# Hybrid decoder step: projections of the scan stage as products of rounded parts, the weights split by transfers

## The chip, the cores and the metric
One core of one Trainium2 chip. The metric is the time of one execution on the device in microseconds (us), lower is better. The engines are called TensorE (PE in the profile, PEld for its weight loads), VectorE (DVE), ScalarE (ACT), GpSimd (POOL) and SyncE (SP). Each works through its own program in order and waits on semaphores.

## The reference
One layer of a hybrid decoder for 512 prompt tokens and 8 x 4 sample tokens, all float32. The input is projected once by `w_in`. Three branches follow (latent attention, a Mamba-2 scan, cross-attention to 256 memory tokens), then a gated merge, and a feed-forward part with 4096 hidden units. The change touches the projections of the scan branch:
```
proj = x @ w_in                     # x: 544 tokens x 1024
z, xbc, dt, ...  = split(proj)      # z: 2048 columns, xbc: 3072
xbc = silu(causal_conv(xbc))        # 4 taps
y, S = ssd(xbc, dt, state)          # chunks of 128 tokens, 4 groups of 8 heads
y = rms_norm_by_group(y * silu(z))
```

## The kernel before, in words
**Layout.** Tokens lie along the free dimension (T = 544, in two halves of HT = 272), features along the 128 partitions. x is `X`, eight chunks of 128 features (KC = 8). The weights come as a stream of 217 blocks of 128 x 1024 (512 KB), in the order in which TensorE uses them (PHASES, line 127; lay_out, line 2441): one for dt, six for the convolution of group 0, then 40 in the stage "ssm" (ten for each of four groups: four of z, six of the next group's xbc, in the last group those of the attention's latents), then mem_k, the heads and so on. SP loads them into `ring`, four slots (load, line 574); a slot is reloaded when TensorE has begun the block after the one in it (`blocks_begun`).

**Two ways of a projection.** `project` (line 1825) multiplies one block with X in float32: 8 chunks x 2 halves, 16 matmuls. `three_products` (line 1840) works with a high part of weights and x, rounded to fp32r, and a low part, the rest: high x high, high x low, low x high, 48 matmuls of a shorter kind. The heads' stage and the merge and feed-forward stages already work by parts: ScalarE rounds a block (round_head_block, line 743), VectorE or GpSimd subtract it from the whole (rest_of_head_block, line 1545; split_block, line 540). The 40 blocks of the scan stage don't.

**The order in the scan stage** is written out by hand on each engine, one loop over the groups each. TensorE (line 2012) has the ten projections in turns with the group's other matmuls: transposes, B by C, states, the read-outs of four pairs of heads (`read_out`), the samples, the state sums (`state_adds`). Blocks are numbered 0 to 9 in a group in what follows: the read-outs stand ahead of blocks 4, 5, 7 and 8. ScalarE (line 829) evacuates z (`z_read`), makes the decays of heads 0 to 7 (`decays`), evacuates the next group's projections (`ahead`), applies tanh (`ahead_silu`) and squares. VectorE (line 1347) convolves, weights the decays (`weigh`), reads the scan's results and adds the sample states (`add_state`). GpSimd (line 478) scales C by the decays (`scale_c`), multiplies eight sample states and sums squares. The rows of cumulated dt come by SP.
```
                for h in range(4):
                    scale_c(h)
                pool.wait_ge(sem["s_off_ready"], t.next("s_off_ready"))
                for b in range(DEC_BATCH):
                    pool.tensor_tensor(by_head(st_s[:, b, :]), by_head(st_s[:, b, :]), heads(dec_s, b, g, P),
                            MUL).then_inc(sem["st_dec_ready"], 1)
                    if b == 3:
                        scale_c(4), scale_c(5)
```

## Time and profile before
| | us |
|---|---|
| median of three timed runs (lowest to highest) | 1672.19 (1671.03 to 1673.26) |
| the profiled execution | 1671.78 |
| its span, first to last instruction | 1669.7 |
| TensorE busy | 1623.7 (97%) |
| VectorE busy | 781.7 (47%) |
| ScalarE busy | 453.3 (27%) |
| GpSimd busy | 407.7 (24%) |

The times come from the whole execution; a profile's rows are of one execution. Busy time of TensorE overlaps from matmul to matmul, so the distance between starts tells more than the mean of one. A row of the timeline merges neighbouring instructions of one line, and its bracket tells how long the engine stood idle before it and what released it. "issue" is time in which it waited for nothing that the profile shows. A float32 matmul leaves two records.

### The profile page before, as it was taken

To read this page: it belongs to the slowest core of one execution; us is meant where nothing else is said; L and a number is where in the kernel's file an instruction comes from. 1 tells how busy PE (TensorE), PEld (TensorE's weight loads), DVE (VectorE), ACT (ScalarE), POOL (GpSimd) and SP (SyncE) were. 2 spreads that over 40 slices of the span, in tenths; PEclk is the share of its full clock that TensorE was granted. 3 is DMA by queue.
4 is the path that set the end of the run, shared out by engine and by line. 5 is a ranking of instruction groups with operands and counts; after the bars stand their busy time and mean duration, and the time that the engine had idled before them with its cause. 6 is when DMAs were issued, how large, how long until landed. Compare 5 with 4: busy or idle time off the path is not lost.

```text
span 1669.7 us, 27037 instructions
## 1 busy us (share of the span) xinstructions
PE 1623.7 (97%) x10950; PEld 1408.9 (84%) x10950; DVE 781.7 (47%) x1350; ACT 453.3 (27%) x857; POOL 407.7 (24%) x344
## 2 busy tenths in 40 slices
PE   8999999999999999999999999999988999999995
PEld 6878787787878888888888877789988999999995
DVE  5657676765343222223333223253488751077234
ACT  2252433425332222222122111142234111111122
POOL 0041231403120000001244200124444334444432
PEclk9999999999999999999999999999999999999998
DMA  5424234252362222224788766422322323222221
GB/s 182 160 78 165 95 114 140 84 184 82 101 231 64 76 76 76 64 76 149 255 273 272 247 246 246 174 89 89 93 72 64 89 89 88 86 84 86 88 64 54
DMA packets 71853, 210.62 MB, mean 126 GB/s; under 512 B 10321, under 2 KB 26962, under 8 KB 66866
## 3 DMA queue, kind: packets, MB, share of 16 engines
q1 hardware_dynamic: 51824, 155.99, 29.5%
q10 hardware_dynamic: 13762, 31.93, 5.4%
q0 software_dynamic: 6144, 20.98, 3.5%
q8 instruction: 86, 1.41, 0.3%
q14 instruction: 37, 0.30, 0.1%
HBM read 194.01 MB, written 14.86 MB: 125 GB/s over the span
## 4 chain that ended last, share of the span: by engine, by line
PE 84%; DVE 7%; ACTq 3%; ACT 2%; issue 2%; DMA 1%; SPq 0%; POOL 0%; DVEq 0%
PE acc L1902 30%; PE acc L1835 21%; PE acc L1848 9%; PE acc L2208 4%; PE acc L2171 3%; PE acc L2154 2%; ACTq L1014 1%; ACTq L1012 1%; PE bank L2222 1%; PE bank L2241 1%; PE bank L2223 1%; DVE work L1303 1%; PE bank L2294 1%; PE bank L2326 1%; PE bank L2189 1%
## 5 line engine op out<-in xcount | busy, mean ns | idle before, releaser
L1835 PE MATMUL acc<-xt,ring 128*128 128x272 f32 x1504 | 358.9, 395 | 0.0
L1835 PEld LDWEIGHTS acc<-xt,ring 128*128 128x128 f32 x1504 | 282.4, 190 | 67.7 <-issue 12.0
L1902 PE MATMUL acc<-x_parts,f_parts 128*128 128x272 f32 x1408 | 219.6, 291 | 10.7 <-DVE x_parts L1230 6.2
L544 POOL TENSOR_TENSOR f_parts<-ring,f_parts 128x1024 fp32r<-128x1024 f32 x65 | 158.5, 2439 | 247.2 <-ACT f_parts L764 247.0
L1902 PEld LDWEIGHTS acc<-x_parts,f_parts 128*128 128x128 f32 x1408 | 196.0, 191 | 13.4 <-issue 6.0
L1902 PE MATMUL acc<-f_parts 128*128 128x272 f32 x1344 | 172.3, 289 | 0.0
L522 POOL DMA_DIRECT2D work<-in_page_cols x128 | 69.0, 539 | 422.2 <-PE bank L2262 382.0
L1902 PEld LDWEIGHTS acc<-f_parts 128*128 128x128 f32 x1344 | 170.4, 188 | 0.1
L1848 PE MATMUL acc<-work_high,high 128*128 128x272 f32 x464 | 138.4, 298 | 0.0
L764 ACT ACTIVATE f_parts<-ring 128x1024 fp32r<-128x1024 f32 x65 | 68.8, 1059 | 239.2 <-PE acc L1902 204.5
L1848 PE MATMUL acc<-work_high,ring_low 128*128 128x272 f32 x464 | 133.8, 288 | 0.0
L1848 PE MATMUL acc<-x_low,high 128*128 128x272 f32 x384 | 110.7, 288 | 0.0
L1848 PEld LDWEIGHTS acc<-work_high,high 128*128 128x128 f32 x464 | 87.2, 188 | 5.7 <-issue 5.3
L1848 PEld LDWEIGHTS acc<-work_high,ring_low 128*128 128x128 f32 x464 | 87.7, 189 | 0.0
L1549 DVE TENSOR_TENSOR ring_low<-ring,high 128x1024 fp32r<-128x1024 f32 x32 | 39.2, 1224 | 86.7 <-ACT high L749 86.4
L1798 DVE TENSOR_SCALAR f_parts<-attended 128x544 fp32r<-128x544 f32 x32 | 76.5, 2390 | 1.1
L1848 PEld LDWEIGHTS acc<-x_low,high 128*128 128x128 f32 x384 | 73.0, 190 | 0.2 <-issue 0.2
L1303 DVE SCALAR_TENSOR_TENSOR work<-work,vecs 128x600 f32<-128x600 f32 x72 | 68.5, 951 | 2.4
L1902 PE MATMUL acc<-f_parts,mg_parts 128*128 128x272 f32 x528 | 68.8, 289 | 0.0
L544 POOL TENSOR_TENSOR mg_parts<-ring,mg_parts 128x1024 fp32r<-128x1024 f32 x21 | 51.0, 2426 | 70.8 <-ACT mg_parts L764 70.8
L1902 PEld LDWEIGHTS acc<-f_parts,mg_parts 128*128 128x128 f32 x528 | 67.3, 188 | 0.2
L1902 PE MATMUL acc<-x_parts,mg_parts 128*128 128x272 f32 x480 | 62.1, 289 | 0.6 <-DVE attended L1792 0.6
(369 smaller groups left out, 2508.7 us busy)
## 6 DMA issues: line engine op xcount, KB each, us to landing
ring<-in_stream SPq DMA_DIRECT2D x216, 512.0 KB, 3.6
work<-in_page_cols POOLq DMA_DIRECT2D x128, 160.0 KB, 5.1
attended<-in_ssm_state ACTq DMA_DIRECT2D x8, 1024.0 KB, 6.3
work<-cum_rows SPq DMA_DIRECT2D x32, 256.0 KB, 4.5
out_ssm_s<-attended ACTq DMA_DIRECT2D x8, 1024.0 KB, 5.6
work<-in_ckv_rows ACTq DMA_DIRECT2D x64, 128.0 KB, 3.6
work<-in_ckv_rows SPq DMA_DIRECT2D x64, 128.0 KB, 2.6
work<-in_memk_cols SPq DMA_DIRECT2D x8, 1024.0 KB, 7.2
```

The source lines that it names most:

```text
L522: pool.dma_start(keys[kq][:, i * KEYS_W:(i + 1) * KEYS_W], page_cols[ids[kq * 4 + i]]).then_inc(sem[f"keys_in_slot{kq}"], 16)
L544: pool.tensor_tensor(lo, ring[:, s * BLOCK:(s + 1) * BLOCK], hi.bitcast(F), SUB).then_inc(sem["split_ready"], 1)
L764: act.activation(hi, ring[:, s * BLOCK:(s + 1) * BLOCK], ACT.Copy).then_inc(sem["hi_ready"], 1)
L1303: dve.scalar_tensor_tensor(out=c, in0=ext[j][:, i:i + CL], scalar=tap(i), in1=c, op0=MUL, op1=ADD).then_inc(sem[signal], 1)
L1549: dve.tensor_tensor(ring_low[:, of], ring[:, of], W_HIGH[i % 2].bitcast(F), SUB).then_inc(sem["split_ready"], 1)
L1798: dve.tensor_scalar(hi, q, 1.0, None, MUL).then_inc(sem["dve_step"], 1)
L1835: m = pe.matmul(acc[p][:, half, 0:width], w[:, k * P:(k + 1) * P], x(kk)[:, half * width:(half + 1) * width], start=kk == 0, stop=kk == n_ ...
L1848: m = pe.matmul(out[:, half, 0:HT], w[:, k * P:(k + 1) * P], x[k][:, of], start=k == 0 and n == 0, stop=last and k == KC - 1 and n == 2)
L1902: m = pe.matmul(acc_half, w[:, k * P:(k + 1) * P], x[:, kk, of], start=kk == 0 and n == 0, stop=kk == last and n == 2)
L2154: m = pe.matmul(acc[p][:, 0, 0:N_MEM], w[:, k * P:(k + 1) * P], mem[:, k, :], start=k == 0, stop=k == KC - 1)
L2171: m = pe.matmul(acc[p][:, half, 0:HT], w[:, c * 256 + off:c * 256 + off + P], cq[:, c, half * HT:(half + 1) * HT], start=c == 0, stop=c == 2)
L2208: m = pe.matmul(acc[1][:, half, 0:HT], w[:, k * P:(k + 1) * P], BR[:, KC + k, half * HT:(half + 1) * HT], start=False, stop=k == KC - 1)
```

## The change
The 40 blocks of the scan stage are multiplied by parts (`project_parts_of_x`). Their weights are split by transfers, which GpSimd issues. Of block i the stream is moved once into a slot of `ring_parts` (fp32r, at the place of `ring`) by a transfer that rounds; ScalarE writes the negative of the rounded block to one of three buffers W_LOW; a second transfer adds the stream to it, which leaves the low part. The adding transfer of block i+2 is issued ahead of the rounding one of block i+3, at ten places in GpSimd's program, and the negations stand at ten places in ScalarE's. x is rounded and its rest subtracted in place at the start of the stage and no more at its end. SP loads nothing into the ring in the stage, and loads mem behind it. Semaphores are merged.
```diff
+            def round_weights(i):
+                at = SSM_AT + i
+                s = at % RING
+                if i < SSM_SPLIT:
+                    pool.wait_ge(sem["blocks_begun"], CREDIT["blocks_begun"] + at - RING + 2)
+                    pool.dma_start(ring_parts[:, s * BLOCK:(s + 1) * BLOCK], stream[at]).then_inc(sem[f"w_rounded{i % 2}"], 16)
+
+            def rest_of_weights(i):
+                if i < SSM_SPLIT:
+                    if i:
+                        pool.wait_ge(sem["w_rest"], 16 * i)
+                    pool.wait_ge(sem["negated"], i + 1)
+                    pool.dma_start(W_LOW[i % 3], stream[SSM_AT + i], accum_op=ADD).then_inc(sem["w_rest"], 16)
+
+            def weights_ahead(g, q):
+                i = g * (GC + QC) + q
+                rest_of_weights(i + 2)
+                round_weights(i + 3)
+
+            round_weights(0)
+            rest_of_weights(0)
+            round_weights(1)
+            rest_of_weights(1)
+            round_weights(2)
             for g in range(GROUPS):
...
                 pool.wait_ge(sem["const_loaded"], 2 * 16)
+                weights_ahead(g, 0)
                 pool.wait_ge(sem["conv_ready"], t.next("conv_ready", QC))
...
+                weights_ahead(g, 1)
+                weights_ahead(g, 2)
                 pool.wait_ge(sem["cb_read"], t.next("cb_read"))
...
+                weights_ahead(g, 3)
                 for h in range(4):
                     scale_c(h)
+                weights_ahead(g, 4)
                 pool.wait_ge(sem["s_off_ready"], t.next("s_off_ready"))
...
                     if b == 3:
                         scale_c(4), scale_c(5)
+                weights_ahead(g, 5)
                 scale_c(6), scale_c(7)
+                weights_ahead(g, 6)
                 pool.wait_ge(sem["sq_ready"], t.next("sq_ready", 2))
                 pool.tensor_tensor(zc[0], zc[0], zc[1], ADD).then_inc(sem["pool_step"], 1)
+                weights_ahead(g, 7)
+                weights_ahead(g, 8)
...
                 pool.tensor_tensor(sq_sum, zc[0], zc[2], ADD).then_inc(sem["sq_added"], 1)
+                weights_ahead(g, 9)
...
+            block_at.next(SSM_SPLIT)
+            load(3)
+            begun_behind(SSM_AT + SSM_SPLIT - 2)
+            sp.dma_start(mem, mem_t).then_inc(sem["mem_loaded"], 16)
...
+            def negate(i):
+                s = (SSM_AT + i) % RING
+                if i < SSM_SPLIT:
+                    act.wait_ge(sem[f"w_rounded{i % 2}"], 16 * (i // 2 + 1))
+                    if i >= 3:
+                        act.wait_ge(sem["blocks_begun"], CREDIT["blocks_begun"] + SSM_AT + i - 3 + 2)
+                    act.activation(W_LOW[i % 3], ring_parts[:, s * BLOCK:(s + 1) * BLOCK].bitcast(F), ACT.Copy,
+                            scale=-1.0).then_inc(sem["negated"], 1)
...
+                negate(first + 2)
                 z_read(0)
+                negate(first + 3)
...
                 z_read(1)
+                negate(first + 4)
                 z_read(2)
+                negate(first + 5)
...
                 z_read(3)
+                negate(first + 6)
...
                 ahead(0)
+                negate(first + 7)
                 act.wait_ge(sem["y_ready"], t.next("y_ready"))
                 decays(4)
                 decays(5)
...
                 decays(6)
                 ahead(1)
+                negate(first + 8)
                 decays(7)
...
                 ahead(2)
+                negate(first + 9)
                 ahead_silu(2)
                 ahead(3)
+                negate(first + 10)
                 square(2)
...
                 ahead(4)
+                negate(first + 11)
                 square(3)
...
             conv(0, 4)
             finish(0, 3)
...
+            for c in range(KC):
+                if c < KC - 1:
+                    dve.wait_ge(sem["x_read"], c + 1)
+                else:
+                    dve.wait_ge(sem["acc0_ready"], 1 + QC // 2)
+                rest_of_chunks(XL, X, XH, (c,))
             conv(0, 5)
             finish(0, 4)
...
+            def project_parts_of_x(p, between=None):
+                pe.wait_ge(sem[f"acc{p}_free"], t.next(f"acc{p}_free"))
+                s, i = (used.next() - 1) % RING, split_in_ssm.next() - 1
+                pe.wait_ge(sem["w_rest"], 16 * (i + 1))
+                w_high, w_low = ring_parts[:, s * BLOCK:(s + 1) * BLOCK], W_LOW[i % 3]
+                three_products(acc[p], w_high, w_low, XH, XL, True, 0, None if i else "low_even")
+                if between:
+                    between()
+                m = three_products(acc[p], w_high, w_low, XH, XL, True, 1)
+                m.then_inc(sem[f"acc{p}_ready"], 1)
```

## Rows read from the trace of the kernel before

**Rows 1.** The page: busy us, share of the span and instructions of each engine.
```profile
PE 1623.7 (97%) x10950; PEld 1408.9 (84%) x10950; DVE 781.7 (47%) x1350; ACT 453.3 (27%) x857; POOL 407.7 (24%) x344
```

**Rows 2.** Stages, one group: busy us (count) by engine, granted clock, DMA share, GB/s.
```profile
257.50:355.80 98.30, 97.56 (x554) 76.73 (x553) 70.20 (x119) 38.42 (x86) 25.23 (x21) 1.00 0.36 122
```

**Rows 3.** Waits in that group: engine, line, releaser, us in total, times, longest.
```profile
POOL work L508 <- ACT work L902: 21.0, 1, 21.0
ACT work L838 <- PE acc L1835: 19.1, 4, 7.3
```

**Rows 4.** Timeline of TensorE, ahead of the first read-out (start, us, line, shape, [idle before]).
```profile
297.42 0.66 PE L2075 MATMUL bank<-work 128*64 128x128 f32 x8 [0.56 <-DVE work L1401]
```

**Rows 5.** Timeline of TensorE: two and a half float32 projections, and what follows.
```profile
246.50 18.50 PE L1835 MATMUL acc<-xt,ring 128*128 128x272 f32 x80
264.83 1.08 PE L2008 MATMUL bank<-work,cst 128*128 128x272 f32 x4
```

**Rows 6.** Timeline of TensorE in the feed-forward stage: two projections by parts.
```profile
1339.80 12.24 PE L1902 MATMUL acc<-x_parts,f_parts 128*128 128x272 f32 x96
1351.88 6.20 PE L1902 MATMUL acc<-x_parts,mg_parts 128*128 128x272 f32 x48
```

**Rows 7.** Landing: ring loads (512 KB), mem (1024 KB); GpSimd's issues (ns) and landing (160 KB).
```profile
DMA to landing us min/median/max: 3.4/3.6/12.3
...
DMA to landing us min/median/max: 4.9/4.9/4.9
...
L522 POOL DMA_DIRECT2D work<-in_page_cols x128: 536/538/707, 480.2 to 941.5; - x128
...
DMA to landing us min/median/max: 2.7/5.1/8.2
```

**Rows 8.** ScalarE's rounding (ns min/median/max); the group's scalings (busy, mean ns); timeline.
```profile
L749 ACT ACTIVATE high<-ring x32: 1041/1049/1062, 499.9 to 957.6; 128x1024 fp32r<-128x1024 f32 x32
...
L494 POOL TENSOR_TENSOR work<-work 128x384 f32<-128x384 f32 x8 | 8.8, 1102 | 17.7 <-ACT work L858 17.7
...
309.39 1.27 ACT L854 ACTIVATE work<-work 128x128 f32<-128x128 f32 x4
...
313.47 0.51 ACT L858 ACTIVATE work<-work 128x384 f32<-128x384 f32 x1
...
314.06 1.21 POOL L494 TENSOR_TENSOR work<-work 128x384 f32<-128x384 f32 x1 [1.02 <-ACT work L858]
315.23 4.50 POOL L500 TENSOR_TENSOR attended<-attended,work 128x512 f32<-128x512 f32 x4
```

**Rows 9.** Timeline of GpSimd: the sums of squares at a group's end.
```profile
251.70 1.49 POOL L508 TENSOR_TENSOR work<-work 128x544 f32<-128x544 f32 x1 [20.92 <-ACT work L902]
253.27 1.76 POOL L512 TENSOR_TENSOR work<-work 128x544 f32<-128x544 f32 x1
```

**Rows 10.** The DMA view of the same group: all that moved.
```profile
DMA packets 3598, 11.98 MB, mean 122 GB/s; under 512 B 640, under 2 KB 640, under 8 KB 3072
```

**Rows 11.** Timeline of VectorE: last convolution of group 0; four low parts of x.
```profile
60.04 0.18 DVE L1313 SCALAR_TENSOR_TENSOR branch<-work 128x32 f32<-128x32 f32 x1
...
63.20 0.17 DVE L1291 TENSOR_SCALAR work<-work 128x3 f32<-128x3 f32 x1 [2.77 <-ACT work L781]
...
64.12 2.60 DVE L1303 SCALAR_TENSOR_TENSOR work<-work,vecs 128x600 f32<-128x600 f32 x3
...
460.62 2.62 DVE L1543 TENSOR_TENSOR x_low<-xt,work_high 128x544 fp32r<-128x544 f32 x4
```

**Rows 12.** Timeline: two weightings, two state sums; TensorE's block 7 begins.
```profile
326.43 1.29 DVE L1401 TENSOR_TENSOR work<-work 128x512 f32<-128x512 f32 x2
327.64 1.28 DVE L1462 TENSOR_TENSOR attended<-attended,bank 128x512 f32<-128x512 f32 x2
...
330.24 3.83 PE L1835 MATMUL acc<-xt,ring 128*128 128x272 f32 x16
```

**Rows 13.** Timeline of TensorE: what follows the stage's last projection.
```profile
453.28 2.92 PE L1873 MATMUL bank<-work,cst 128*128 128x272 f32 x12
```

More of the change, by code:

```diff
@@ L143 @@
 HEAD_SPLIT = len(SPLIT_AT)
+SSM_AT = blocks_before("ssm")
+SSM_SPLIT = GROUPS * (GC + QC)
 def loaded_before(block, slot):
-    return len(range(slot, block, RING))
+    return sum(not SSM_AT <= at < SSM_AT + SSM_SPLIT for at in range(slot, block, RING))
 CREDIT = {"acc0_free": 1, "acc1_free": 1, "blocks_begun": 8, "keys_used": 4,
@@ L278, in program @@
         ext, cacc, th = ([k(EXT) for _ in range(2)] for _ in range(3))
-        krope, a_rstd = k(T), k(T)
-        late_sq = [k(T) for _ in range(2)]
-        k_rstd = late_sq[0]
+        low_at = k.at
+        krope = work[:, low_at:low_at + T]
+        x_high_at = low_at + BLOCK
+        k.at = low_at + 4 * T
+        assert x_high_at + 2 * T <= k.at
         after_conv = k.at
@@ L289, in program @@
         bc = [k(2 * T).rearrange("p (c t) -> p c t", t=T) for _ in range(2)]
+        cum_at = k.at
         cum_r = [k(SEQ) for _ in range(4)]
+        a_rstd, k_rstd = (work[:, cum_at + i * T:cum_at + (i + 1) * T] for i in range(2))
         b_last = work[2 * NS:NS3, k.at:k.at + P]
@@ L312, in program @@
         xw_full = xdt[NS:2 * NS, NB, :]
-        mem = k(KC * N_MEM).rearrange("p (c m) -> p c m", m=N_MEM)
+        x_high_too_at = k.at
+        k(3 * T)
+        mem = spare[:, 0:KC * N_MEM].rearrange("p (c m) -> p c m", m=N_MEM)
+        mem_again = work[:, xdt_at:xdt_at + KC * N_MEM].rearrange("p (c m) -> p c m", m=N_MEM)
         decay = [xw[:, c, :] for c in range(NB)]
@@ L359, in program @@
         for_heads = k.at
-        a_sq = [bc[0][:, 0, :], bc[0][:, 1, :], late_sq[0], late_sq[1], work[:, b_tm_at:b_tm_at + T]]
+        a_sq = [bc[0][:, 0, :], bc[0][:, 1, :], *(work[:, late_sq_at + i * T:late_sq_at + (i + 1) * T] for i in range(2)),
+                work[:, b_tm_at:b_tm_at + T]]
+        assert late_sq_at + 2 * T <= cum_at - 4 * T
         q_n = k(T)
@@ L794, in latent @@
                 act.activation(a_sq[i], dst, ACT.Square).then_inc(sem["squares_ready"], 1)
+            for c in range(0, KC, 2):
+                act.wait_ge(sem[f"x{c // 2}_loaded"], 32)
             evac(1)
+            round_chunks(XH, X, range(2))
             evac(0)
@@ L805, in _ @@
                               ssm_state[0][:, 4 * i:4 * i + 4, :]).then_inc(sem[f"st{i}_loaded"], 16)
-            act.dma_start(mem, mem_t).then_inc(sem["mem_loaded"], 16)
+            round_chunks(XH, X, range(2, 4))
             evac(0)
             silu(1)
-            act.wait_ge(sem["wb_ready"], t.next("wb_ready"))
+            negate(0)
+            round_chunks(XH, X, range(4, 6))
+            act.wait_ge(sem["cum_ready"], 2)
             act.activation(wb_tm[:, 0:NB, :], wb_tm[:, 0:NB, :], ACT.Exp)
@@ L813, in _ @@
             act.activation(dec_s, bank[0][:, 0:DEC_BATCH * SSM_HEADS].rearrange("p (b h) -> p b h", h=SSM_HEADS),
-                    ACT.Exp).then_inc(sem["dec_ready"], 1)
+                    ACT.Exp).then_inc(sem["exps_ready"], 1)
             evac(1)
+            round_chunks(XH, X, range(6, KC))
+            negate(1)
             silu(0)
@@ L1345, in _, with rest_of_chunks @@
             finish(0, 3)
+            def rest_of_chunks(low, whole, high_parts, cs):
+                for c in cs:
+                    dve.wait_ge(sem["rounded"], t.next("rounded"))
+                    dve.tensor_tensor(low[c], whole[:, c, :], high_parts[c].bitcast(F), SUB).then_inc(sem["low_even"], 1)
+            for c in range(KC):
[4 more added lines that the diff above has]
+                rest_of_chunks(XL, X, XH, (c,))
             conv(0, 5)
@@ L1534, in variance @@
                 m.then_inc(sem[signal], 1)
-            variance(a_rstd, lambda half: bank[half], "cq_summed", Q_LORA, "var_ready")
+            variance(a_rstd, lambda half: bank[half], "latent_summed", Q_LORA, "var_ready")
             group_var()
-            variance(k_rstd, lambda half: acc[0][:, half, :], "ckv_summed", KV_LORA, "var_ready")
-            def rest_of_chunks(low, whole, high_parts, cs):
-                for c in cs:
-                    dve.wait_ge(sem["rounded"], t.next("rounded"))
-                    dve.tensor_tensor(low[c], whole[:, c, :], high_parts[c].bitcast(F), SUB).then_inc(sem["low_even"], 1)
+            variance(k_rstd, lambda half: acc[0][:, half, :], "latent_summed", KV_LORA, "var_ready")
             def rest_of_head_block(i):
@@ L1839, in project @@
                                 m.then_inc(sem["blocks_begun"], 1)
+                            elif half and read and k < KC - 1:
+                                m.then_inc(sem[read], 1)
+                m.then_inc(sem[f"acc{p}_ready"], 1)
[8 more added lines that the diff above has]
+                m = three_products(acc[p], w_high, w_low, XH, XL, True, 1)
                 m.then_inc(sem[f"acc{p}_ready"], 1)
@@ L2061, in _ @@
                 states(0, 1)
-                project(0, of_x, between=lambda: states(2, 3))
+                project_parts_of_x(0, between=lambda: states(2, 3))
                 def read_out(hp):
```

127 lines of the change are left out of this document (60 added, 67 removed).

## The prediction

> **What bounds the kernel now.** I read the page first: TensorE is busy for 97% of the span [rows 1]. Then the stretch of the change, the scan stage (four groups of ten projections), by the view of stages: one group lasts 98.3 us, TensorE is busy for 97.5 of them, VectorE for 70, ScalarE for 38, GpSimd for 25, and the DMA engines for 0.37 [rows 2]. The granted clock is 1.00, the 2.4 GHz level. So here the stage lasts as long as TensorE's work, and every other engine waits: GpSimd up to 21.0 us at a time, ScalarE 19.1 us in a group for z's projections [rows 3]. TensorE itself waits once in a group, 0.56 us, for VectorE's weighting of the decays [rows 4].
>
> **The matrix products.** Two and a half plain projections in a row take from 246.50 to 264.83 [rows 5]: 7.33 us for one of 16 float32 matmuls (each has two records). Two projections as three products of parts, 96 matmuls, take from 1339.80 to 1351.88 [rows 6]: 6.04 us for one. Forty projections so save 40 x 1.29 = 51.6 us of TensorE's time. That is the most the change can bring. What it puts at stake is the supply of the weights, which today is one plain load per block, 3.6 us to landing against a block time of 9.8 [rows 7].
>
> **The new supply, as a chain.** Per block GpSimd issues two software transfers (one rounds 512 KB into ring_parts, one adds the same 512 KB to the negated copy), and ScalarE negates in between. Their order on GpSimd is: wait for `negated(i)`, add(i), round(i+1). ScalarE's negate(i+1) waits for round(i+1). So add(i) cannot start before negate(i), round(i+1) stands behind it on one queue, and negate(i+1) behind that: from one negation to the next it takes L + 1.3 us. L is the time from the issue of the adding transfer to the landing of the rounding one behind it. 1.3 is the negation (ScalarE took 1.05 us to round a block of the same size) and 0.25 for three hand-overs, of about 0.08 each (ScalarE's exponential ends 313.98, GpSimd starts 314.06) [rows 8]. Three buffers allow the chain to run ahead, but never make it quicker than one block in L + 1.3.
>
> **What else stands in that chain.** Both engines work in program order, and the new steps stand between old ones. Per group:
> - between negations 5 and 6: negation 6 waits until block 4 has begun, and block 4 stands behind decays 0 and 1, their scaling and the first read-out: 0.4 + 4.6 + 1.1 + 1.7 = 7.8, which is 1.3 more than L if L is 6.5;
> - between 6 and 7: round(7) stands behind scale_c(3) on GpSimd, that behind decays 2 and 3 on ScalarE, these behind negate(6). A pair of decays takes 4.6 us (309.39 to 313.98), a scaling 1.1 on average [rows 8]: 5.7 us;
> - between 7 and 8: decays 4 and 5 (4.6 us), scale_c(5) 1.2, and then the last four state products, 4.5 us, before weights_ahead(5) issues round(8): 10.3 us [rows 8];
> - between 8 and 9: decay 7 and scale_c(7), 2.3 + 1.2 = 3.5 us;
> - between 11 and 12: square(3) 0.7, the sums 1.5 + 1.7 on GpSimd: 3.9 us [rows 9].
> Together 24.7 us. With ten steps of L + 1.3 a group takes **10 L + 37.7** us, wherever that is above what TensorE needs. What TensorE needs is 98.3 - 12.9 = 85.4, plus 0.7 for the wait on VectorE (its part from the read-outs of states 2 and 3 to the weighted decays is fixed work, so half a projection less of cover makes the 0.56 longer): 86.1.
>
> **Bounds of L.** The trace has no adding and no rounding transfer. Rows near it: 512 KB land in 3.6 us, 1024 KB in 4.9 with nothing beside, so 512 KB more cost 1.3 and the fixed part is 2.3; a 160 KB transfer issued by GpSimd landed at best in 2.7, which is the same 2.3 with its issue [rows 7]. If a transfer that adds moves no more than a plain one, the pair is 1 MB: L = 2.3 + 2.6 = 4.9. If reading the old values counts as much again, the pair is 1.5 MB: 2.3 + 3.9 = 6.2. The stage also moves 11.98 MB in a group, 5.24 of it the loads that the pairs replace [rows 10]; the other 6.7 MB are some 17 us of 98, so the data part grows by about a quarter: 5.5 and 7.2. Nothing excludes that the arithmetic itself is slower than plain copying; by no row can I bound that above, and I let it reach 8. I take 6.6, nearer to the upper case, since `accum_op` has to fetch the old contents and the rounding one shares its queue.
> The Trainium skill, Collectives: The Full Stack, section "The bandwidth ceiling", says that a transfer with a reduction runs at half the rate of a copy, because both sources are read on one ring, and not because the addition costs time. No row here shows it; by it L would be the 7.2 of the paragraph above.
> The Trainium skill, SBUF — State Buffer, warns in its note on "DVE blocks DMA" that GpSimd can't write descriptors while VectorE holds the port pair they share. The issues that the trace shows took 0.54 us at the median and 0.71 at most, so here it would add 0.2 us to an issue, 8 us over 40 blocks at the most, inside the bounds of L.
>
> **The sum.** Start: VectorE makes the low parts of x behind finish(0,3), which ends at 60.2; eight of 0.66 us (2.62 for four) end at 65.5, so the last convolution of the first group starts there instead of at 63.2 and its last tap ends at 69.0; tanh 0.7 and the negation give 71.0 for negate(2) of group 0 [rows 11]. TensorE waits for the same: the low parts cost it some 1 us at its first block, the convolution about as much behind it, both inside the 71.0. Then three groups, 3 x (10 L + 37.7); then from negate(2) to negate(8) of the last, 6 L + 7.8 + 1.3 + 5.7 + 10.3 = 6 L + 25.1 (six steps of L + 1.3, and the first three of the extras); then VectorE: decay 7 to its exponential 1.9, its weighting 0.65, two state sums 1.25, two matmuls 0.6 = 4.4 us to block 7 (VectorE has weigh(7) ahead of add_state(0), for which TensorE waits) [rows 12]; then blocks 7 to 9, 330.24 to 355.80 less 3 x 1.29 = 21.7. The stage's projections end at 36 L + 235.3. They end at 453.28 now [rows 13]. With L = 6.6 that is 472.9: **19.6 us later**. Zero is at L = 6.05.
>
> **Edits at nothing.** The 40 ring loads leave SP's queue; behind them stand the loads of the cumulated rows, which can only come earlier. The load of mem leaves ScalarE's queue for SP's, behind the last block's begin; needed 7 us later, and 1024 KB land in 4.9 [rows 7]; if the queue is full it costs up to 2. The rounding of x at the end (ScalarE 2.9 us, VectorE 3.2) stood beside TensorE's sums behind 453.28 and its mem_k blocks: removed for nothing. The parts of BR move under the same blocks; 8 x 0.66 on VectorE at their end, first needed 20 us later. The second load of mem and shared semaphores change no order that matters. If each of these costs 1 us, that is 3, within the range.
>
> **Base.** The profiled execution ran 1671.8 us with a span of 1669.7; the median of the three timed runs is 1672.2. The forecast is 1671.8 + 19.6 = 1691.4.
>
> **Rivals.**
> 1. The other side: adding costs little more than copying, L of 4.9 to 5.9, and the time is below now. At L = 5.5 the sum gives 1671.8 - 20 = 1652; below 5.4 the chain stops counting in part (from negate(8) the way over block 7, 8, 9, the evacuation and the convolution to negate(12) is 34 us whatever L). One mechanism, one point: L under 6.05. For it: the DMA engines are busy for only 0.37 of the stage now [rows 2]. Against: every old transfer of the stage shares them. 0.25.
> 2. The supply is hidden whole: L under 4.6, or GpSimd and ScalarE run further ahead than I think. Then TensorE's 86.1 per group rules: 51.6 - 4 x 0.7 - 2.5 at the start = 46 us saved, 1626; with some rest 1640. Against: a pair needs 4.9 by the cheapest rows. 0.10.
> 3. The transfers with arithmetic are much slower than plain ones, L of 8 to 10: 1742 to 1814. No row speaks for or against. 0.15.
> 4. L between 6.0 and 6.15: no difference that counts. 0.06.
> 5. That the change doesn't do what it says (the transfer doesn't round, so the parts are no parts) would alter results, not this time: the matmuls and transfers are the same.
>
> **How the numbers follow.** Forecast, L of 6.15 to 7.6 (1675 to 1728): 0.44. A measurement of this kernel tells 0.2%, 3.3 us, from no change. Faster is rivals 1 and 2, 0.35; same 0.06; slower the forecast and rival 3, 0.59. The two signs share the chance, so the range reaches from the middle of the fast cases, 1640, to L of 8, 1743, and leaves out most of rival 2 and the tail of 3. The likeliest case's own range is 1675 to 1728.
>
> **What would show it.** Matmuls of the stage 126 ns apart where they run: 6.04 per block. Right if TensorE's idle time before blocks 4 to 9 is released by DMA or by VectorE's state sums, ScalarE's longest waits are for the rounding transfer ahead of its negations, GpSimd's for the negation, and a group lasts about 104 us. Wrong if groups last 86 to 90 with no idle time on TensorE (L small), if the landing of the adding transfer alone is above 7 us (L large), if the granted clock falls in the gaps (a cost that I have at nothing, as it stays at 1.00 over the present gaps), or if the idle time sits at conv_ready, which would make VectorE the bound.

## The result, and the profile after

The changed kernel took 1728.78 us (median of 4 runs, 1727.48 to 1734.93) against 1672.7 us before on the same chip: a ratio of 1.0344, 95% interval 1.0322 to 1.0366. So 56 us slower, where 19.6 were forecast. Slower was the likeliest sign and the range (1640 to 1743) holds the time, but the forecast's own case (to 1728) ends just under it, and the size is nearly three times what the sum gave.

The profiled execution of the changed kernel took 1734.93 us (span 1732.0); it is 6 us above the other three, which lie within 1.3 us of each other. All that follows is read from it. The page, the same parts as [rows 1], with the chain that ended last:
```profile
PE 1602.9 (93%) x11590; PEld 1436.4 (83%) x11590; DVE 799.3 (46%) x1350; ACT 491.3 (28%) x897; POOL 461.7 (27%) x424
...
PE 66%; DMA 12%; issue 6%; ACT 5%; POOL 5%; DVE 4%; ACTq 3%; POOLq 0%; SPq 0%; DVEq 0%
PE acc L1992 29%; DMA ring_parts<-in_stream 11%; PE acc L1938 9%; PE acc L1912 7%; PE acc L2298 3%; PE acc L2261 3%; POOL work L540 2%; PE acc L2244 2%; ACTq L1089 1%; ACTq L1087 1%; ACT work L923 1%; PE bank L2312 1%; POOL attended L548 1%
```
TensorE's share fell from 97% to 93%, and the landing of the rounding transfer is now 11% of the chain. Where the stage's projections end, TensorE's timeline shows the sum that follows them (L1963 here, 453.28 in [rows 13]):
```profile
515.25 1.09 PE L1963 MATMUL bank<-work,cst 128*128 128x272 f32 x4
```
That is 62.0 us later, and the span grew by 62.3 (1669.7 to 1732.0): the loss lies up to the end of this stage. Behind it the time moved by 0.3 us, so what was costed at nothing there cost next to nothing.

The stages of the same kernel, the stretch that answers to [rows 2] (us, then busy us and count of each engine, granted clock, DMA share, GB/s):
```profile
171.00:278.00 107.00, 82.99 (x644) 74.55 (x643) 67.28 (x105) 45.28 (x92) 36.67 (x39) 0.87 0.53 138
278.00:385.00 107.00, 86.19 (x661) 77.88 (x660) 73.17 (x114) 46.39 (x94) 37.41 (x40) 0.90 0.57 150
```
No engine is full now. TensorE has 21 to 24 us of idle time in 107, and its granted clock, 1.00 before, is 0.87 and 0.90. Who waits for whom, from 60 to 530 us (engine, what waits, releaser, us in total, times, longest):
```profile
ACT high L835 <- DMA ring_parts<-in_stream: 127.5, 22, 9.9
POOL high L509 <- ACT high L835: 118.1, 16, 11.3
...
ACT work_high L835 <- DMA ring_parts<-in_stream: 61.9, 11, 8.8
POOL work_high L509 <- ACT work_high L835: 57.4, 8, 8.9
...
PE bank L2165 <- POOL work L540: 30.9, 4, 8.7
...
PE bank L2206 <- DVE attended L1548: 24.0, 7, 10.4
```
ScalarE's negations (L835) wait for the rounding transfer, GpSimd's adding transfers (L509) for the negation: the chain of the forecast. TensorE hardly ever waits for a weight itself. It waits for the read-out's scaled C (L2165) and for the state sums (L2206), because ScalarE's decays and GpSimd's scalings stand in program order behind the transfers' steps. From negation 2 to 12, to 22 and to 32 the groups last 113.8, 115.8 and 113.6 us, where about 104 were forecast.

Two steps of that chain, from negation 19 to negation 21 of 40. First GpSimd's queue (L509 adding, L502 rounding), then ScalarE's (L835 negation):
```profile
270.82 0.90 POOL L509 DMA_DIRECT2D high<-in_stream  x1 [7.67 <-ACT high L835]
271.42 0.86 POOL L502 DMA_DIRECT2D ring_parts<-in_stream  x1
279.01 0.88 POOL L509 DMA_DIRECT2D high<-in_stream  x1 [6.73 <-ACT high L835]
```
```profile
269.20 1.06 ACT L835 ACTIVATE high<-ring_parts 128x1024 fp32r<-128x1024 f32 x1 [7.71 <-DMA ring_parts<-in_stream]
...
277.41 1.06 ACT L835 ACTIVATE high<-ring_parts 128x1024 fp32r<-128x1024 f32 x1 [2.00 <-DMA ring_parts<-in_stream]
...
279.00 0.35 ACTq L891 DMA_DIRECT2D out_ssm_s<-attended  x1
...
287.76 1.06 ACT L835 ACTIVATE work_high<-ring_parts 128x1024 fp32r<-128x1024 f32 x1 [3.98 <-DMA ring_parts<-in_stream]
```
Negation at 269.20, adding transfer 1.62 later at 270.82, next negation 6.59 after that: a step of 8.21 us with nothing beside it. The next step begins at 277.41; at 279.00 a 1 MB store of the states starts beside it, and the negation comes 8.75 us after the adding transfer. These two are the two kinds of step that the stage has. L, from the adding transfer's start to the landing of the rounding one behind it, read so for the 36 steps from negation 2 to negation 38: 6.56 to 6.81 us in 17 of them (the quiet ones in what follows), 7.07 to 9.53 in the others, **7.49 in the mean**.

### The profile page after: what moved, and what is told of

Its sections match the earlier page's. It is cut to its first block, busy times and chain, and to the rows that moved or that the text cites. A ratio compares the mean times of both kernels' runs of the same rounds, so it can differ in the third digit from the quotient of the medians.

```text
span 1732.0 us, 28478 instructions
## 1 busy us (share of the span) xinstructions
PE 1602.9 (93%) x11590; PEld 1436.4 (83%) x11590; DVE 799.3 (46%) x1350; ACT 491.3 (28%) x897; POOL 461.7 (27%) x424
## 4 chain that ended last, share of the span: by engine, by line
PE 66%; DMA 12%; issue 6%; ACT 5%; POOL 5%; DVE 4%; ACTq 3%; POOLq 0%; SPq 0%; DVEq 0%
PE acc L1992 29%; DMA ring_parts<-in_stream 11%; PE acc L1938 9%; PE acc L1912 7%; PE acc L2298 3%; PE acc L2261 3%; POOL work L540 2%; PE acc L2244 2%; ACTq L1089 1%; ACTq L1087 1%; ACT work L923 1%; PE bank L2312 1%; POOL attended L548 1%; PE bank L2331 1%; PE bank L2313 1%
## 5 line engine op out<-in xcount | busy, mean ns | idle before, releaser
L1938 PE MATMUL acc<-work_high,ring_parts 128*128 128x272 f32 x768 | 225.8, 294 | 0.0
L1938 PE MATMUL acc<-x_low,ring_parts 128*128 128x272 f32 x640 | 191.4, 299 | 0.0
L1938 PE MATMUL acc<-work_high,high 128*128 128x272 f32 x628 | 184.4, 294 | 0.0
L1938 PEld LDWEIGHTS acc<-work_high,ring_parts 128*128 128x128 f32 x768 | 149.4, 194 | 0.6 <-DVE x_low L1425 0.4
L1938 PEld LDWEIGHTS acc<-x_low,ring_parts 128*128 128x128 f32 x640 | 128.4, 201 | 2.3 <-issue 1.2
L1938 PEld LDWEIGHTS acc<-work_high,high 128*128 128x128 f32 x628 | 121.0, 193 | 0.0
L1938 PE MATMUL acc<-high,ring_parts 128*128 128x272 f32 x256 | 82.4, 322 | 4.7 <-DMA high<-in_stream 2.7
L1630 DVE TENSOR_TENSOR ring_parts<-ring,high 128x1024 fp32r<-128x1024 f32 x32 | 39.2, 1224 | 88.5 <-ACT high L800 88.2
L835 ACT ACTIVATE high<-ring_parts 128x1024 fp32r<-128x1024 f32 x26 | 27.6, 1060 | 135.8 <-DMA ring_parts<-in_stream 127.5
```

The lines of the kernel that those rows point to most:

```text
L1630: dve.tensor_tensor(ring_parts[:, of], ring[:, of], W_HIGH[i % 2].bitcast(F), SUB).then_inc(sem["split_ready"], 1)
L1938: m = pe.matmul(out[:, half, 0:HT], w[:, k * P:(k + 1) * P], x[k][:, of], start=k == 0 and n == 0, stop=last and k == KC - 1 and n == 2)
```

## The experiments

"End" is the time at which the stage's projections end in a run's profile (453.28 before, 515.25 changed; elsewhere the first weight load of the same sums, which reads 515.1 in the changed kernel). Mean L and the other terms are over the same 36 steps throughout. A time given as of one run has no interval; the four runs of the changed kernel lie 7 us apart.

**Which price makes L.** Three runs change one size each.

The second transfer doesn't add:
```
-  pool.dma_start(W_LOW[i % 3], stream[SSM_AT + i], accum_op=ADD)
+  pool.dma_start(W_LOW[i % 3], stream[SSM_AT + i])
```


> The changed kernel, with the second transfer of each block writing rounded weights in place of adding to the negated ones (the low parts are then wrong: the addition is left out, all transfers, waits and bytes written stay). Theory A1, the sum of reading and writing back in an adding transfer is a large term of L: L falls from 6.6 (quiet) by 1 to 2 us, the whole by 36 times that: 1655 to 1695 us. Rival A2, an adding transfer costs what a rounding one does: L within 0.3 us of 6.6, 1720 to 1740.

Measured: 1688.52 us (one run), end 470.8. Quiet steps have L = 5.0 to 5.3 (changed kernel: 6.6 to 6.8), the mean is 5.99 in place of 7.49. Theory A1 in its size: adding, in place of writing the rounded weights, costs some 1.6 us of a quiet step. Whether the fetching of the old contents or the arithmetic takes them, the run does not tell. The sum of L fell by 54.0 us and the end by only 44.3, since the waits behind the landings, nearly all for TensorE (a buffer becomes free when a block has begun), grew from 11.7 to 22.9 us in all.

The adding transfer moves half a block:
```
-  pool.dma_start(W_LOW[i % 3], stream[SSM_AT + i], accum_op=ADD)
+  pool.dma_start(W_LOW[i % 3][:, 0:BLOCK // 2], stream[SSM_AT + i][:, 0:BLOCK // 2], accum_op=ADD)
```


> The changed kernel, with the adding transfer moving only the first half of each block's columns (256 KB in place of 512; the other half of the low parts stays the negated rounded weights). If L is bytes through the engines (two transfers of 512 KB in 6.6 us, some 5 us of it bytes), it falls by a quarter of them, 1.2 to 1.7 us a step: 1670 to 1690 us. If L is the fixed latency of the rounding transfer behind, and the adding one runs beside it, it stays within 0.4 us: 1715 to 1735.

Measured: 1698.39 us (one run), end 483.1; quiet L about 6.1, mean 6.67. Neither case: half of the adding bytes gives 0.5 us of a quiet step, 0.8 of the mean. The two transfers overlap in part, and the one that L ends with is the rounding one.

The transfers by themselves, behind the last work of the kernel before (`one` issues a transfer, `landed` waits for it):
```
+  for _ in range(3):
+      one(parts[0]), landed()
+  for _ in range(3):
+      one(parts[0], accum_op=ADD), landed()
+  ...
+  for _ in range(3):
+      one(parts[0], accum_op=ADD), one(parts[1]), landed()
```


> The kernel before, with transfers alone behind its last store, when every engine is idle (the outputs are the kernel's own): from GpSimd's queue one block each, waited for: three rounding, three adding, one of each of 256 KB; three pairs adding + rounding issued together, three pairs rounding + rounding; then all but the halves again while SyncE's queue loads blocks of 512 KB one after the other into other memory; at the end two plain ones. If the changed kernel's quiet landings (5.4 adding, 6.1 rounding behind it, 6.6 for the pair) are the price of the transfers themselves, the bare pair takes 6.4 to 6.8 us and beside plain loads 7.5 to 9; rounding + rounding takes 5.0 as where the addition was left out. If instead half of it is the stage's own traffic, the bare pair takes under 5.8 us. A single rounding one: 3.5 to 4.5 us; a single adding one 4.5 to 5.4. The whole about 200 us longer than the kernel before: 1860 to 1900.

Measured: 1867.78 us (one run). GpSimd's timeline; a row's bracket is the wait for the landing of the transfer ahead of it: a rounding transfer, two adding ones, a rounding and an adding one of 256 KB, two adding + rounding pairs; then, beside SyncE's loads, two such pairs more.
```profile
1671.76 0.53 POOL L573 DMA_DIRECT2D ring_low<-in_stream  x1 [3.46 <-DMA ring_low<-in_stream]
...
1685.94 0.89 POOL L573 DMA_DIRECT2D ring_low<-in_stream  x1 [4.84 <-DMA ring_low<-in_stream]
1691.68 0.88 POOL L573 DMA_DIRECT2D ring_low<-in_stream  x1 [4.85 <-DMA ring_low<-in_stream]
1697.49 0.55 POOL L573 DMA_DIRECT2D ring_low<-in_stream  x1 [4.93 <-DMA ring_low<-in_stream]
1700.83 0.86 POOL L573 DMA_DIRECT2D ring_low<-in_stream  x1 [2.78 <-DMA ring_low<-in_stream]
1705.38 1.46 POOL L573 DMA_DIRECT2D ring_low<-in_stream  x2 [3.68 <-DMA ring_low<-in_stream]
1712.35 1.42 POOL L573 DMA_DIRECT2D ring_low<-in_stream  x2 [5.51 <-DMA ring_low<-in_stream]
...
1791.73 1.43 POOL L573 DMA_DIRECT2D ring_low<-in_stream  x2 [10.00 <-DMA ring_low<-in_stream]
1803.22 1.43 POOL L573 DMA_DIRECT2D ring_low<-in_stream  x2 [10.06 <-DMA ring_low<-in_stream]
```
From issue to landing the rounding ones took 3.8 to 3.9 us, the adding ones 5.5; of 256 KB 3.1 and 4.2. So rounding costs 0.8 us for the second 256 KB and adding 1.3. The bare pair takes 6.97 us from one issue to the next (1705.38 to 1712.35), of which 0.3 is the way from a landing to the next issue (1691.68 less 1685.94 is 5.74, and that adding transfer landed after 5.46). L, read to the landing, is 6.7 to 6.9 bare, no less than in a quiet step of the stage; two rounding ones take 5.2 to 5.4, near the 5.0 to 5.3 where the addition was left out. **So the quiet L is the price of these transfers, and no traffic of the stage.** Beside plain loads, which with it keep the DMA engines 0.93 busy, the pair takes 10.2 to 11.2 us (the longest from 1791.73), more than the 7.5 to 9 expected.

**What makes the other steps longer.** The transfers of the states cut to a sixteenth, and then those of the cumulated rows too:
```
-  act.dma_start(st_s[:, 4 * i:4 * i + 4, :], ssm_state[g][:, 4 * i:4 * i + 4, :])
+  act.dma_start(st_s[:, 4 * i:4 * i + 1, 0:GW // 4], ssm_state[g][:, 4 * i:4 * i + 1, 0:GW // 4])
   (the store of the new states likewise)
```


> The changed kernel, with the loads and stores of the sample states (4 samples of 128x512, 1 MB each, four of them a group) cut to one sixteenth of their bytes (states of groups 1 to 3 are not loaded and new states not stored whole; waits and issues stay). Theory D, L is 6.6 us alone and 7 to 9 beside these transfers, and the step of the forecast that failed is the share of blocks beside them: the mean L falls from 7.8 to 6.6-6.9, 36 times that off the end: 1685 to 1700 us. Rival E, the long landings come from something else (the rows of cumulated decays, the packets of the queue itself): within 8 us of the changed kernel, 1720 to 1740.

Measured: 1718.48 us (one run), end 499.7, mean L 7.14. The blocks beside the states fell (block 3 of groups 1 to 3 from 9.16, 8.71 and 8.75 to 6.86, 7.19 and 6.77), but the mean fell by 0.34 and not by 1. The time fell by 10 us from the median, 16 from the profiled run: it lies between the two cases.

```
+  n = SEQ if pair < 2 else 32
-  sp.dma_start(cum_r[...], cum_d[h:h + 1, 0:SEQ].broadcast_to([P, SEQ]))
+  sp.dma_start(cum_r[...][:, 0:n], cum_d[h:h + 1, 0:n].broadcast_to([P, n]))
```


> The changed kernel in its own order, with both other traffics of the stage made small: the sample states as in e4_small_states, and from the second pair of heads on only 32 of the 512 columns of each row of cumulated decays (the exponentials of the other columns are then taken of nothing; waits and issues stay). Theory D (all landings beyond 6.6-6.9 us come from transfers beside them): the landings that stayed at 7.4 to 9.7 us in e4_small_states, those of blocks 8 and 0 of a group, fall to 6.6-7.0 too, the mean from 7.14 to 6.7-6.85, 10 to 16 us off the end: 1700 to 1708 us. Rival E (the queue's own unevenness): the long ones stay, 1714 to 1720.

Measured: 1714.84 us (one run), end 495.4, mean L 7.05. The time is in rival E's case, and 3.6 us under the run before, which single runs can't tell from none. Theory D is right for the states; for the rest it is not shown: at blocks 8, 18 and 28 the landings stayed long (L 8.63, 8.05, 9.75; 9.56, 7.45 and 9.71 with the states' cut alone). The DMA view of this kernel, from 251 to 261 us, says what is beside block 18's:
```profile
DMA packets 848, 1.11 MB, mean 111 GB/s; under 512 B 592, under 2 KB 592, under 8 KB 848
...
q0 software_dynamic: 288, 1.05, 45.7%
q1 hardware_dynamic: 560, 0.07, 4.1%
```
The shortened rows are only 0.07 MB, but still 560 packets, against 288 of the software queue. That the number of small packets, not their bytes, holds up the transfer is a reading that fits; it was not tried by itself, and what makes these landings long stays open.

**The chain: order and places.** The rounding transfer ahead of the adding one:
```
-  rest_of_weights(i + 2)
   round_weights(i + 3)
+  rest_of_weights(i + 2)
```


> The changed kernel, with the rounding transfer of block i+3 issued ahead of the adding transfer of block i+2 (nothing of the computation changes). Theory A, the chain add -> round -> negate: the negation and its hand-over (1.06 + 0.55 us a block) and the program places of the negations no longer stand between two transfers, a block needs only what two transfers back to back need (6.6 to 7.9 us), less than TensorE's 8.6, so the groups fall from 113-117 us to 86-98 and the end of the stage's projections from 515 to 440-460: 1640 to 1690 us. Rival B, the queue itself is full (two transfers of 512 KB cannot pass in less than the 8.3 us that a quiet step takes): groups stay above 105, 1715 to 1740. Rival C, TensorE's lowered clock sets the time: 1715 to 1740 too, but with its idle time before the weights' waits unchanged.

Measured: 1683.56 us median, ratio to before 1.0069 (1.0048 to 1.0091), 45 us under the changed kernel; end 464.0. Theory A, at the slow end of its time; the end is 4 us beyond its 460, and the groups, 99.9 and 99.5 us (negations 12 to 22 to 32), just beyond its 98. Rival B (the queue is full) is out: the same transfers pass at a DMA share of 0.69 and 0.68 in the two stretches, where it was 0.53 and 0.57. While GpSimd waits for the negation, the next block's rounding transfer is already on its way.

The original order, with three adding transfers earlier in GpSimd's program:
```
-  for h in range(4): scale_c(h)
-  weights_ahead(g, 4)
+  scale_c(0), scale_c(1)
+  weights_ahead(g, 4)
+  scale_c(2), scale_c(3)
   ...
       if b == 3:
+          weights_ahead(g, 5)
           scale_c(4), scale_c(5)
-  weights_ahead(g, 5)
-  scale_c(6), scale_c(7)
+  scale_c(6)
   weights_ahead(g, 6)
+  scale_c(7)
```


> The changed kernel in its own order (adding transfer ahead), with three of its adding transfers issued at other places of GpSimd's program: that of block 6 of a group between the second and the third scaling of C (it stood behind all four), that of block 7 ahead of the fifth (it stood behind eight state products and two scalings), that of block 8 between the last two scalings. Theory A (the time from a negation to its adding transfer, 6.7, 10.7 and 4.4 us at these blocks against 1.6 at the others, is GpSimd's program and lies on the chain): they fall to about 1.6, 7 and 1.6, some 11 us a group off the chain, 36 to 45 in all: 1685 to 1700 us. Rival F (these places wait for TensorE's and ScalarE's work of the group, which will end as late as before): under 10 us gained, 1720 to 1735.

Before this edit the changed kernel's GpSimd worked so between negations 26 and 28 (which start at 338.08 and 368.96):
```profile
344.79 0.89 POOL L509 DMA_DIRECT2D high<-in_stream  x1
...
345.95 4.35 POOL L548 TENSOR_TENSOR attended<-attended,work 128x512 f32<-128x512 f32 x4
354.89 1.52 POOL L540 TENSOR_TENSOR work<-work 128x384 f32<-128x384 f32 x1 [4.59 <-ACT work L927]
...
358.21 4.07 POOL L548 TENSOR_TENSOR attended<-attended,work 128x512 f32<-128x512 f32 x4
362.23 0.88 POOL L509 DMA_DIRECT2D work_high<-in_stream  x1
```
Negation 26 was done at 339.14 and its adding transfer went out at 344.79; negation 27 (351.50) is followed by its own at 362.23, behind four state products and two scalings. These delays are 6.7 and 10.7 us in every group (in the last one the second is 12.1), in every run that keeps the order and the places, whatever L is. Measured with the edit: 1687.91 us, ratio 1.0087 (1.0067 to 1.0107), 41 us less; end 470.4. Over the 36 steps the time from a negation to its adding transfer fell from 133.8 to 70.8 us, and the waits behind the landings rose from 11.7 to 31.4: of 63 us taken off the chain 45 came through, the rest is spent waiting until TensorE frees a buffer.

Both edits:

> Both edits of the transfers' version: rounding transfer ahead of the adding one, and the three adding transfers at the earlier places. Theory A: with the chain broken by the order, the places matter little more; what is left is bytes in the queue and TensorE: 1665 to 1684 us, 0 to 18 us under the swap alone (1683.6). If the places and the order gained independently it would fall to 1640 to 1650.

Measured: 1657.88 us, ratio 0.9930 (0.9907 to 0.9954): 14 us **under the kernel before**. End 439.9. The expectation that the places would matter little once the order was turned was wrong: they gave another 26 us, less than the 41 that they gave alone. They delay not only the chain but the adding transfer itself, which TensorE's block needs; that this is what the 26 us are is a reading, no run parts the two.

And the transfers of a group's last place, moved in front of GpSimd's last two sums of squares:
```
   weights_ahead(g, 8)
+  weights_ahead(g, 9)
   pool.wait_ge(sem["sq_ready"], t.next("sq_ready", 2))
   ...
-  weights_ahead(g, 9)
```


> c2_swap_places (1657.9 us) with the transfers of the last place of a group issued ahead of GpSimd's last two sums of squares in place of behind them: the 11 us landings of blocks 0 and 1 of the next group begin earlier. If TensorE's waits there (2.4 to 2.5 us twice, and the pace of 96.5 us a group) come from them, 1 to 3 us a group: 1648 to 1656. If c2 is bound by TensorE's need and clock: 1655 to 1660.

Measured: 1654.46 us (1653.44 to 1655.09), ratio 0.9894 (0.9878 to 0.9911), the best version, 17.5 us under the kernel before. By itself the fourth place gave 3.4 us, and the intervals of the two ratios touch, so its own share is not clear of noise. TensorE's waits from 60 to 440 us and the stage's stretches:
```profile
PE bank L2166 <- DVE work L1488: 7.5, 4, 2.1
PE bank L2207 <- DVE branch L1566: 7.4, 3, 2.7
PE bank L2207 <- DVE attended L1549: 5.5, 4, 1.5
...
PE acc L1939 <- DMA high<-in_stream: 1.7, 3, 0.8
...
171.00:278.00 107.00, 100.38 (x834) 91.64 (x834) 82.41 (x135) 55.99 (x108) 42.50 (x45) 0.98 0.76 194
278.00:385.00 107.00, 97.62 (x786) 88.14 (x785) 83.25 (x132) 55.67 (x113) 43.42 (x46) 0.97 0.69 174
```
TensorE is busy again for 98 to 100 of 107 us, the transfers cost it 1.7 us in all, and VectorE has taken their place as what it waits for.

**Without the supply, and with another one.** Only the first four blocks are rounded and the first three negated and added to; TensorE waits for no later one, and its products take what lies in the buffers:
```
-  if i < SSM_SPLIT:      (in round_weights, rest_of_weights, negate)
+  if i < RING:           (rounding)         if i < 3:   (adding, negation)
```


> The changed kernel without its supply: only the first four rounding and the first three negated and adding transfers are made, every later block multiplies with what lies there (the projections from block 3 on are wrong; all products, read-outs, state updates and their waits stay). It gives the floor of the products by parts in this stage. Theory A (the forecast's need of TensorE, 86.1 us a group, is right, at a clock near 1.00): the stage's projections end at 410 to 425, the whole at 1626 to 1640. Rival G (read-outs and state adds, or the clock, don't let the stage go under 95 a group): end at 445 or later, 1660 or more.

Measured: 1634.01 us (one run). The stage's end, its stretches, and one group from first state sum to first state sum:
```profile
L1966 PEld LDWEIGHTS bank<-work,cst x12: 187/188/193, 416.9 to 419.3; 128*128 128x128 f32 x12
...
171.00:278.00 107.00, 101.22 (x836) 91.03 (x835) 87.74 (x141) 47.38 (x109) 30.39 (x24) 1.00 0.19 63
278.00:385.00 107.00, 102.87 (x860) 93.06 (x856) 76.58 (x125) 48.64 (x113) 35.91 (x30) 0.98 0.22 78
...
121.20:211.03 89.83, 85.11 (x715) 77.20 (x713) 72.27 (x119) 38.39 (x86) 27.30 (x22) 1.00 0.22 75
```
Theory A: TensorE is busy for 85.0 to 86.5 us of a group, where 86.1 were forecast as its need. A group lasts 88.6 to 90.6, for TensorE still waits for VectorE now and then. The changed kernel is 95 us above this floor, and all of that goes when the supply goes.

The supply by engines: one plain load a block by SyncE as before, ScalarE rounds where it negated, GpSimd subtracts where it issued the adding transfer:
```
-  pool.dma_start(W_LOW[i % 3], stream[SSM_AT + i], accum_op=ADD)
+  pool.tensor_tensor(ring_parts[slot], ring[slot], W_LOW[i % 3].bitcast(F), SUB)
```


> The products of parts as in the changed kernel, but no weights through GpSimd's queue: SyncE loads each block once as in the kernel before, ScalarE rounds it where it negated (same places), and GpSimd subtracts in place (low = weights - rounded) at the places where it issued the adding transfer, about 2.4 us each. Theory A (the loss is the transfers' chain, not the products by parts): TensorE's own need, about 86 us a group, or GpSimd's 27 + 24 us and its order, set the stage, and it ends at 400 to 430 us: 1625 to 1650. Rival G (the products by parts can't be fed in this stage whatever fills the weights, since read-outs and state adds come late and the clock falls): 1665 to 1700.

Measured: 1685.87 us, ratio 1.0091 (1.0074 to 1.0108). In the time of rival G, but not for its reason, since the run without supply refutes it. VectorE is busy for 91.0 and 91.5 us in the two stretches, where 73.6 and 73.5 were used for about as many instructions in the run with the places alone (121 in both, and 122 against 120). GpSimd's timeline and VectorE's beside it:
```profile
216.41 2.38 POOL L506 TENSOR_TENSOR ring_parts<-ring,high 128x1024 fp32r<-128x1024 f32 x1
...
231.50 2.57 POOL L506 TENSOR_TENSOR ring_parts<-ring,high 128x1024 fp32r<-128x1024 f32 x1
```
```profile
216.75 2.08 DVE L1366 TENSOR_SCALAR work<-work 128x24 f32<-128x24 f32 x1
...
231.90 2.80 DVE L1380 SCALAR_TENSOR_TENSOR work<-work,vecs 128x600 f32<-128x600 f32 x1
...
254.20 0.17 DVE L1366 TENSOR_SCALAR work<-work 128x24 f32<-128x24 f32 x1
```
The same small VectorE instruction takes 0.17 us alone and 2.08 beside a subtraction, and ends (218.83) when that ends (218.79). A convolution tap, 0.84 us alone, takes 2.80. The Trainium skill, SBUF — State Buffer, section "SBUF: two separate sides", says that GpSimd and VectorE share a pair of ports, and that of a GpSimd instruction and a VectorE one which needs the pair too (two inputs in SBUF, or one of its faster two-port modes) the first to start holds it for its whole instruction; these rows agree. With the subtractions at the earlier places:

> c1_engines (one plain load a block, ScalarE rounds, GpSimd subtracts) with the subtractions of blocks 6, 7 and 8 of a group at the earlier places of e6_places. Theory A (c1 lost to late subtractions behind GpSimd's own work): PE's waits go and it falls by 10 to 30 us, 1656 to 1676. Theory H (c1 lost because GpSimd's 24 us of subtractions a group slow VectorE, 91.0 us busy in 107 against 73.6 at the same count): within 8 us of c1's 1685.9, or slower, since the scalings of C come later.

Measured: 1680.51 us, ratio 1.0047 (1.0031 to 1.0064), 5.4 under the former, with VectorE nearly as busy (89.9 and 90.8 us). Theory H. It is 22.6 us slower than the transfers with both edits. TensorE's waits from 60 to 440 us:
```profile
PE bank L2210 <- DVE branch L1568: 15.2, 3, 6.0
PE bank L2210 <- DVE attended L1551: 9.0, 4, 3.5
```
With the smaller ones they are 43 us for VectorE and none for a weight; with the transfers and both edits 25 us for VectorE and 6 for the transfers. So what the transfers are worth here is that they keep VectorE less. They don't leave it alone altogether. VectorE in the changed kernel, beside an adding and a rounding issue (344.79 to 346.23) and the four state products behind them, which end at 350.30:
```profile
345.14 5.20 DVE L1364 TENSOR_SCALAR work<-work 128x24 f32<-128x24 f32 x1
```
In the two groups ahead the same instruction beside the same issues took 0.91 us, still five times the 0.17 of one alone. Whether the issues or the products held it, the rows don't tell.

## Why the prediction was right and wrong

**Right: what the change is bound by.** The chain, its members and its order are those forecast: the waits of ScalarE and GpSimd, and where TensorE's idle time falls. The formula, the stage's end = 36 L + 235.3, with the measured mean L of 7.49 gives 504.9 for 515.25. TensorE's need (86.1 a group, busy for 85.0 to 86.5 without the supply) and the end of negation 2 (71.0, measured 71.53) held too.

**Wrong: the size of L.** The term that failed is "I take 6.6": L measured 7.49. The end came 42.4 us later than the 472.9 forecast:
- L: 36 x (7.49 - 6.6) = +32.0 us, three quarters of the miss. The price of the bare pair was too low: it was put between 4.9 and 6.2, and it is 6.7 to 6.9, already more than the 6.6 taken with the stage's traffic. Two rounding transfers take 5.2 to 5.4 where 4.9 stood for two plain ones. Reading the old values was priced as 512 KB more, 1.3 us; adding costs 1.6 (5.5 less 3.9), some 1.0 of it by the slope (1.3 against 0.8 us for 256 KB) and 0.6 as a fixed part. The traffic was not priced too low in the mean: the forecast gave it 0.6 to 1.0 us, and the mean L is 0.7 above the bare pair. But it comes in lumps, next to nothing in half of the steps and up to 2.9 us in the others.
- The steps outside L: 133.8 from negations to adding transfers and 11.7 of waits behind the landings, 145.5 us where 36 x 1.3 and the extras gave 138.2: +7.3. A plain step has 1.61 in place of 1.3: three hand-overs of 0.08 were put down, but the one from the negation to the transfer's start is 0.55. The extras by place came out somewhat shorter than forecast (for block 7 9.1 over a plain step against 10.3, for block 6 5.1 against 5.7).
- The start, to the end of negation 2: +0.5.
- From the end of negation 38 (486.59) to the stage's end: 28.7 where 26.1 was forecast, +2.6. Block 37 begins at 490.99, 4.4 us behind the negation as forecast; the 2.6 come in blocks 37 to 39, 24.3 us for 21.7. Most of them are the clock's, which I had at nothing. TensorE's timeline at block 37 of the changed kernel:
```profile
489.80 1.39 PE L2206 MATMUL bank<-rounded 96*128 96x512 f32 x2 [10.42 <-DVE attended L1548]
490.99 0.43 PE L1938 MATMUL acc<-high,ring_parts 128*128 128x272 f32 x1
491.21 0.43 PE L1938 MATMUL acc<-x_low,ring_parts 128*128 128x272 f32 x1
...
496.12 0.29 PE L1938 MATMUL acc<-work_high,high 128*128 128x272 f32 x1
496.25 0.64 PE L2206 MATMUL bank<-rounded 96*128 96x512 f32 x2
```
After 10.42 us of idle time the matmuls start 0.22 to 0.23 us apart, the 1.2 GHz level, and only from 496 on 0.13 apart again: 22 of them at about half pace, 2.2 us. The gaps before were 0.56 us, and from those no fall could be read. In the middle of a group the same fall lengthens the wait of block 6's negation (2.5 to 2.9 us where 1.3 was forecast): in the second group the read-out ahead of block 4 takes 3.2 us (219.13 to 222.32; from 217 to 222 the granted clock is 0.50) where one at the full clock takes 1.7 (499.83 to 501.52). What the clock costs in all was not tried by itself. By the rows it is about 2.2 us of the end, and of the waits at block 6, 11.0 us in all, what lies above the forecast, 11.0 - 4 x 1.3 = 5.8 us; these are a part of the +7.3.

Together +42.4 of the profiled run's 43.5 over the forecast; the median of the runs is 37.4 over it.

**The range of the likeliest case.** It ended at L = 7.6, and the mean L of 7.49 lies inside it; by the formula that L alone gives 1723.4. What carried the median just past 1728 are the terms outside L. The rule of the Trainium skill (Collectives: The Full Stack, section "The bandwidth ceiling"), half the rate of a copy, gave L = 7.2 and so an end of 494.5, 20.8 short of the measured one where my 6.6 is 42.4 short. The runs agree with it in part: a second 256 KB costs 1.3 us against 0.8, that is 0.6 of the rate, and 0.6 us of fixed cost come on top, which the rule doesn't have. The note of the Trainium skill, SBUF — State Buffer, on "DVE blocks DMA" changed nothing for the issues: an adding transfer's issue takes 0.86 to 0.91 us in the stage and 0.86 to 0.90 with all other engines idle. The other way round the delay is seen, in the 5.20 us above. One row was read a little off: the DMA share before is 0.36, not 0.37; nothing rests on the difference.

**The rivals.** The first rival has no gain at L = 6.05 and a gain below. With the adding left out L is 5.99 in the mean and the kernel is still 16 us slower than before, so that point lay too high, by the steps outside L and the longer waits for TensorE. The second is out, since the bare pair takes 6.7. The third is out as a cause, for the mean L stayed under its 8, though single steps reached 9.5.

## What to carry to other kernels

When a step of a weight's preparation waits for another engine and its transfers share one in-order queue, issue the next block's first transfer ahead of this block's second: the hand-overs then overlap, and it was worth 45 us here with the same transfers. Look in the issuing engine's program for what stands between the signal and the issue; three moved places were worth another 26, and with a fourth a loss of 3.4% became a gain of 1.1%. And price a transfer that computes by a run of it alone before summing forty of them: in a serial chain each tenth of a microsecond counts once per block.

## What the runs showed of the hardware

- From GpSimd's queue 512 KB took 3.8 to 3.9 us to land when rounding, 5.5 when adding, alone. A pair, adding then rounding, took 6.7 to 6.9; two rounding ones 5.2 to 5.4.
- Beside plain loads of another queue that fill the DMA engines to 0.93 the pair took 10.2 to 11.2 us.
- A VectorE instruction of 24 columns took 2.08 us beside a GpSimd subtraction of 1024 and 0.17 alone. Beside the issues of an adding and a rounding transfer it took 0.91, and 5.20 where four GpSimd products followed on them.
- After idle times of 3.8 to 10.4 us in the changed kernel TensorE's matmuls started 0.22 to 0.23 us apart, the lower level of its clock, for up to 5.0 us of a block; in the run without the supply they did so for 3.4 us after an idle time of 1.54 us.
